# Five RMS norms on per-token sums in three columns, with the reciprocal spread by the tensor engine

## The reference

```python
def rms_norm(x, g):
    xf = x.astype(jnp.float32)
    y = xf * lax.rsqrt(jnp.mean(xf * xf, axis=-1, keepdims=True) + EPS)
    return (y * g.astype(jnp.float32)).astype(x.dtype)
```

## Time and profile before

| | |
|---|---|
| Runs | 2112.90, 2114.68, 2116.01 us; median 2114.68 |
| Profiled execution | 2114.53 us, span 2113.0 us |
| Mean granted clock of TensorE | 0.955 |
| Busy | PE 89%, PEld 81%, DVE 54%, ACT 41%, POOL 3% |
| Chain that ended last, by engine | PE 64%, issue 20%, DVE 10%, ACT 4%, DMA 1% |
| HBM | 115 GB/s over the span |

### The profile page before, as it was taken

How to read it: one execution, slowest core, us unless ns; L and a number is a source line. 1 busy time by engine, 2 the same in 40 slices (tenths; PEclk the granted TensorE clock), 3 DMA queues, 4 the chain that set the end, 5 groups by cost and what they waited for, 6 DMA issues and landing times.

```text
span 2113.0 us, 32355 instructions
## 1 busy us (share of the span) xinstructions
PE 1889.1 (89%) x11226; PEld 1703.9 (81%) x11226; DVE 1134.2 (54%) x1801; ACT 866.5 (41%) x1476; POOL 66.6 (3%) x72
## 2 busy tenths in 40 slices
PE   5977997789999989999989789977899997999995
PEld 3955897559969879999969478966698896999995
DVE  3667545673314477467365755366542246763754
ACT  3444433553322454344354354244533234543432
POOL 1000001000000000000000000011000000000000
PEclk9989999989999999999999899989999999999998
DMA  7410333113324443433353013321132345333331
GB/s 290 155 62 21 120 109 110 40 60 112 130 79 153 173 154 120 159 122 137 140 195 122 33 51 100 127 82 50 63 129 101 130 159 190 104 115 123 126 117 63
DMA packets 55967, 244.41 MB, mean 116 GB/s; under 512 B 6336, under 2 KB 6416, under 8 KB 52016
## 3 DMA queue, kind: packets, MB, share of 16 engines
q1 hardware_dynamic: 49824, 181.43, 25.3%
q0 software_dynamic: 6032, 61.52, 7.4%
HBM read 238.95 MB, written 3.96 MB: 115 GB/s over the span
## 4 chain that ended last, share of the span: by engine, by line
PE 64%; issue 20%; DVE 10%; ACT 4%; DMA 1%; POOL 0%; DVEq 0%; ACTq 0%; POOLq 0%
PE ps L1149 17%; PE ps L1150 17%; PE ps L1151 17%; PE ps L553 2%; PE ps L606 2%; PE ps L582 2%; DVE rstd L1563 1%; PE ps L620 1%; ACT w_hi L1327 1%; DVE wide L1567 1%; ACT region L741 1%; PE ps L473 1%; PE ps L501 1%; DMA region<-in_ada 1%; PE ps L440 1%
## 5 line engine op out<-in xcount | busy, mean ns | idle before, releaser
L1327 ACT ACTIVATE w_hi<-raw 128x1024 fp32r<-128x1024 f32 x344 | 365.0, 1061 | 897.1 <-PE ps L1151 897.1
L1149 PE MATMUL ps<-h_hi,w_hi 128*128 128x384 f32 x1632 | 557.0, 341 | 22.7 <-DVE h_lo L1555 21.9
L1150 PE MATMUL ps<-h_lo,w_hi 128*128 128x384 f32 x1632 | 553.6, 339 | 0.0
L1151 PE MATMUL ps<-h_hi,w_lo 128*128 128x384 f32 x1632 | 553.2, 339 | 0.0
L1551 DVE TENSOR_TENSOR w_lo<-raw,w_hi 128x1024 fp32r<-128x1024 f32 x248 | 327.2, 1319 | 414.0 <-ACT w_hi L1327 409.9
L1149 PE MATMUL ps<-in_hi,w_hi 128*128 128x384 f32 x992 | 344.0, 347 | 52.2 <-DVEq L377 28.4
L1150 PE MATMUL ps<-in_lo,w_hi 128*128 128x384 f32 x992 | 340.8, 344 | 0.0
L1151 PE MATMUL ps<-in_hi,w_lo 128*128 128x384 f32 x992 | 340.4, 343 | 0.0
L1149 PEld LDWEIGHTS ps<-h_hi,w_hi 128*128 128x128 f32 x1632 | 309.7, 190 | 26.8 <-issue 16.8
L1150 PEld LDWEIGHTS ps<-h_lo,w_hi 128*128 128x128 f32 x1632 | 309.9, 190 | 0.5 <-issue 0.3
L1151 PEld LDWEIGHTS ps<-h_hi,w_lo 128*128 128x128 f32 x1632 | 309.6, 190 | 0.0
(11 more groups left out here) (208 smaller groups left out, 1790.8 us busy)
## 6 DMA issues: line engine op xcount, KB each, us to landing
raw<-in_weights SPq DMA_DIRECT2D x346, 512.0 KB, 3.2
region<-in_ada POOLq DMA_DIRECT2D x20, 2048.0 KB, 9.6
wide<-in_ada POOLq DMA_DIRECT2D x2, 1536.0 KB, 7.3
region<-in_ada POOLq DMA_DIRECT2D x2, 1536.0 KB, 7.2
region<-in_consts POOLq DMA_DIRECT2D x2, 1152.0 KB, 5.6
region<-in_state POOLq DMA_DIRECT2D x2, 1024.0 KB, 11.7
region<-in_ada POOLq DMA_DIRECT2D x4, 512.0 KB, 8.5
out_state<-wide POOLq DMA_DIRECT2D x4, 512.0 KB, 2.9
```

Source lines behind the costliest of these rows:

```text
L1149: pe.matmul(out, ah, bh, start=start, stop=False)
L1150: pe.matmul(out, ah, bl, start=False, stop=False)
L1151: m = pe.matmul(out, al, bh, start=False, stop=stop)
L1327: act.activation(w_hi[:, j % AHEAD, :], raw[:, nxt, :], ACT.Copy).then_inc(hi_made.sem, 1)
```

## The change

Norms 1, 4, 5, 6 and 7 get another form; norms 2 and 3 stay. A squared block is now the stationary operand, 128 tokens at a time, and one column of ones streams past it: three matmuls a block, whose sums lie in three PSUM columns, with a token to each partition (`column_sums`). Root and reciprocal are taken on 128x3. Then TensorE multiplies a reciprocal column, broadcast along the free dimension as stationary operand, by the identity, three times 128 columns: this gives every partition the reciprocals of all tokens in a PSUM bank (`spread_rstd`). DVE multiplies with this bank instead of `rstd` in SBUF. Two signals are new, from DVE to TensorE (`rstd_cols_made`) and back (`rstd_spread`); DVE's own chain signal has five links fewer in a layer.

```diff
+        NORM_BANK = {1: 1, 4: 7, 5: 7, 6: 1, 7: 7}
+        def rstd_of(n):
+            return ps[:, NORM_BANK[n], 0:T] if n in NORM_BANK else rstd[:, :]
+        def sums_of(n):
+            return ps[:, NORM_BANK[n], T:T + CHUNKS]
+        root_cols, rstd_cols = stat[:, 0:CHUNKS], stat[:, CHUNKS:2 * CHUNKS]
         mod_cols = ps[:, 4, T:T + 16]
...
         roots = signal("roots", 7)
+        rstd_cols_made = signal("rstd_cols_made", 5)
+        rstd_spread = signal("rstd_spread", 5)
         side_in = [Signal(sem(f"side_in{i}"), 112) for i in range(2)]
...
+        def spread_at(signal_, L, n):
+            return signal_.at(L, (1, 4, 5, 6, 7).index(n) + 1)
         def settle(eng, mark):
...
+            def spread_rstd(L, n):
+                pe.wait_ge(rstd_cols_made.sem, spread_at(rstd_cols_made, L, n))
+                for c in range(CHUNKS):
+                    m = pe.matmul(rstd_of(n)[:, c * P:(c + 1) * P], rstd_cols[:, c:c + 1].broadcast_to([P, P]), ident,
+                                  start=True, stop=True)
+                m.then_inc(rstd_spread.sem, 1)
+            def column_sums(n, i, sq):
+                for c in range(CHUNKS):
+                    m = pe.matmul(sums_of(n)[:, c:c + 1], sq[:, c * P:(c + 1) * P], ones[:, 0:1], start=(i == 0 and c == 0),
+                                  stop=(i == DB - 1), skip_group_check=True)
+                return m
             def added_sum(L, which):
                 pe.wait_ge(added.sem, added.at(L, (which + 1) * (DB - 1)))
-                pe.matmul(ps[:, 7, 0:T], ones, mix[:, 0, :], start=True, stop=True).then_inc(sums.sem, 1)
+                for c in range(CHUNKS):
+                    m = pe.matmul(sums_of(4 + which)[:, c:c + 1], mix[:, 0, c * P:(c + 1) * P], ones[:, 0:1],
+                                  start=True, stop=True)
+                m.then_inc(sums.sem, 1)
+                spread_rstd(L, 4 + which)
...
                     pe.wait_ge(squares.sem, squares_at(L, n, i + 1))
-                    m = pe.matmul(ps[:, 7, 0:T], ones, sq[:, order[i], :], start=(i == 0), stop=(i == blocks - 1))
+                    if n in NORM_BANK:
+                        m = column_sums(n, i, sq[:, order[i], :])
+                    else:
+                        m = pe.matmul(ps[:, 7, 0:T], ones, sq[:, order[i], :], start=(i == 0), stop=(i == blocks - 1))
                     if i == blocks - 1:
                         m.then_inc(sums.sem, 1)
+                if n in NORM_BANK:
+                    spread_rstd(L, n)
...
                 act.wait_ge(sums.sem, sums.at(L, n))
-                act.activation(root[:, :], ps[:, 7, 0:T], ACT.Sqrt, scale=1.0 / width, bias=eps[:, 0:1])\
-                   .then_inc(roots.sem, 1)
+                out, total = (root_cols, sums_of(n)) if n in NORM_BANK else (root[:, :], ps[:, 7, 0:T])
+                act.activation(out, total, ACT.Sqrt, scale=1.0 / width, bias=eps[:, 0:1]).then_inc(roots.sem, 1)
...
                 dve.wait_ge(roots.sem, roots.at(L, n))
-                link(L, dve.reciprocal(rstd[:, :], root[:, :]))
+                if n in NORM_BANK:
+                    dve.reciprocal(rstd_cols, root_cols).then_inc(rstd_cols_made.sem, 1)
+                    dve.wait_ge(rstd_spread.sem, spread_at(rstd_spread, L, n))
+                else:
+                    link(L, dve.reciprocal(rstd[:, :], root[:, :]))
             def times_rstd(n, k, src):
-                dve.tensor_tensor(wide[:, k, :], src[:, k, :], rstd[:, :], ALU.mult).then_inc(scaled_by.sem, 1)
+                dve.tensor_tensor(wide[:, k, :], src[:, k, :], rstd_of(n), ALU.mult).then_inc(scaled_by.sem, 1)
...
-                times_rstd(L, 0, wide)
+                times_rstd(5 + 2 * which, 0, wide)
                 for k in range(DB):
                     if k + 1 < DB:
-                        times_rstd(L, k + 1, wide)
+                        times_rstd(5 + 2 * which, k + 1, wide)
                     dve.wait_ge(scaled_by.sem, scaled_by.at(L, (2 * which + 1) * DB + k + 1))
...
                 for k in range(DB):
-                    times_rstd(L, k, x)
+                    times_rstd(1, k, x)
                 vector(L, 1)
...
                     dve.scalar_tensor_tensor(out=wide[:, k, :], in0=wide[:, k, :], scalar=param("g_ssd", k),
-                                             in1=rstd[:, :], op0=ALU.mult, op1=ALU.mult).then_inc(y_value.sem, 1)
+                                             in1=rstd_of(4), op0=ALU.mult, op1=ALU.mult).then_inc(y_value.sem, 1)
                 y_los(L, 0, lambda k: wide[:, k, :])
...
                 for k in range(DB):
-                    times_rstd(L, k, x)
+                    times_rstd(6, k, x)
                 vector(L, 4)
```

More of the change, by code:

```diff
@@ L107 @@
 DOWN_LAST = ((3, 0, 1, 2, 4, 5, 7, 6), (7, 0, 1, 2, 3, 4, 5, 6))
-DVE_LINKS = 41
+DVE_LINKS = 36
 def build_program(nc, a_x, a_cond, a_state, a_ckv, a_kpe, a_params, a_consts, a_weights, a_ada,
```

## The result

The changed kernel takes 2120.09 us (median of 20 runs) and the kernel before 2111.19 (20 runs beside it); the ratio is 1.0043, 95% interval [1.0031, 1.0055], so the change costs 9.1 us by the ratio, with an interval of 6.5 to 11.6. The profiled execution has 2119.90 us, a span of 2118.3 and a mean granted clock of 0.945 instead of 0.955.

A forecast was written before the change was run, and what follows sets the result against it. TensorE was taken as the bound, a norm counting only through when the next stage's first operand is ready. Terms 5.1 - 4.6 + 3.2 + 6.9 + 1.7 = +12.3 on 2114.68 gave 2127 us, range 2117 to 2136.

The forecast's parts named there:

- Prices: New norm chain 1.5 us at 2.4 GHz, 2.1 at 1.2, against 3.24; new sums cost what the old did at either clock.
- the rival of the fixed time: Weight loads take a fixed time, so sums cost 0.68 us a block at either clock: -3.9, 2111 us; chance 0.04.
- The clock: TensorE loses full clock during column sums: five of norm 7's eight blocks at full clock, three of norm 6's.
- Norm 1, first layer: From the sums to vector 1: slower sums, then columns and sides queued behind the spreading, +5.1 us (0 to +7).
- the sums end at 33.9: Norm 1, first layer: the last three blocks cost 1.3 instead of 0.7 us, so sums end at 33.9, not 31.97.
- Norm 4: Both layers: shorter chain, gate tile fills TensorE's gap, branch's tile ends at 271.0 instead of 273.35: -2.3 us each.
- Norms 5 and 6: Both layers, to vector 4: products come earlier, but columns and side 9 follow the spreading and end last: +1.6 us each.
- Loop: Norm 7 and the next norm 1, to vector 1: slower sums, then sides 2 and 3 behind the spreading: +6.9 us.
- End: Norm 7, second layer, to the last transfer's issue: products later by +1.7 us (-1.4 to +3).
- The rival in which the clock holds: Loads count as activity and column sums keep 2.4 GHz: -9.4, 2105 us, loop still +3.8; chance 0.10.
- the queue behind the spreading: TensorE's columns, sides and first gate tile, queued behind the spreading, now wait for the chain they ran beside; loop +3.8 at full clock.

The follow-up runs named there:

- e3: Changed kernel with 128 columns of ones instead of one behind each weight load in norms 1, 6 and 7: 2097.07 us, ratio 0.9953 to the kernel before.
- e4: Changed kernel with the first group of column matmuls ahead of the spreading in norms 1, 6 and 7: 2114.61 us, ratio 1.0032 to the kernel before.
- e2: Changed kernel with only norms 1, 6 and 7 in the new form, norms 4 and 5 old: 2123.18 us, ratio 1.0089 to the kernel before.
- e6: Changed kernel with norm 1 alone in the new form, all others old: 2117.38 us, ratio 1.0042 to the kernel before.
- e10: Norm 7 alone in the new form, with 128 columns of ones and columns 11 ahead of the spreading: 2113.66 us, ratio 1.0018 to the kernel before.
- e7: On top of e3 and e4, norm 1's side 2 also ahead of the spreading: 2099.01 us, ratio 0.9953 to the kernel before.

## Why the prediction was right, step by step

The forecast of +12.3 us (2127) had the direction and the mechanism; measured were 2120.09, inside the range, and +9.1. Its base, three runs of the kernel before, lay 3.5 us above the median of twenty. Two of its five places came within 0.5 (norm 4, loop); norms 5 and 6 together were 3.0 too dear, norm 1 1.9, the end 0.8 too cheap. Point by point:

- *Prices*: right. The chain is 1.5 us at full clock; a spreading 0.94 or 1.65 (0.91 and 1.5 forecast); a block of column sums 0.67 and 1.28 (0.68 and 1.3 in the sums). Loads start 0.112 apart at full clock and 0.213 at half, so the rival of the fixed time fell. By the Trainium skill, TensorE: Matmul & The Clock Gate, section LDWEIGHTS (loading the stationary operand), a load takes its columns divided by 1.2 in ns, 107 for 128 columns, with no term for the clock. For these f32 records that is near the trace at full clock and half of it at half clock.
- *The clock*: right, and shown by e3: with 128 columns behind each load and the same loads the clock holds at 1.00, and the kernel is 19 us faster than the changed one. Where in the sums it falls was partly luck: three of norm 7's eight blocks were forecast at half clock, 22 of 48 records were (3.7 blocks), 7.80 us against 7.3; the same code took 5.96 in e4.
- *Norm 1, first layer*: +5.1 forecast, +3.2 in the trace and about +2.5 by the ten profiles. The failed step is "the sums end at 33.9": they end at 32.16. The forecast kept the old sums' stretch at half clock (26 to 28) and put three blocks at half clock behind it; in the trace there is one stretch, from 28 on, behind five blocks at full clock. In e2, e4 and e6 the clock fell earlier and the place is at +4.3 to +5.0. Chain, columns and sides behind the sums are as forecast (12.27 from the sums' end to vector 1, 12.4 forecast).
- *Norm 4*: -2.3 forecast, -2.6 and -1.7 measured, by another sum: the products came 1.1 and 1.0 earlier, not 1.7, since the spreading ran at half clock (1.65), and in the first layer the branch's tile gained 1.5, not 0.6, since all of its half-clock stretch fell on the gate tile. The gap of 3.9 us behind the gate tile is gone.
- *Norms 5 and 6*: the mis-sized term, +1.6 each forecast, -0.1 and +0.3 measured. In the first layer the sums themselves took what was forecast (8.48 us from 737.43 to 745.91, 8.5 forecast). They began 5.78 after the fifth sum began instead of 6.67, for columns 7 and side 8 ran partly at full clock (0.5 and 3.25 instead of 0.7 and 3.6); and from their end to vector 4 it took 7.44 instead of 8.2, mainly since columns 9 came at full clock again (0.61 for 1.1). That the columns end last, not the products, was right.
- *Loop*: +6.9 forecast, +7.3 measured, and by the forecast's way: vector 1 waits for the columns of sides 2 and 3, which run behind the spreading, and their loads are there (no wait at 1076.00). The size is luck in part, for two misses cancel: the next reciprocal came 26.2 us after norm 7's sums began, 24.8 forecast and 23.1 before, and the two sides took 5.34 instead of 6.4. What I had not seen is TensorE's own way round the loop; in the changed kernel it lies under the queue, but it alone costs +4.7 with norm 7's sums at full clock (e10). Norm 1's +5.3 (e6) and this +4.7 don't add up to the +7.3; that both wait for the same sides is how I read it, and no run shows it.
- *End*: +1.7 forecast, +2.5 measured: the sums took 2.9 longer, 1.85 forecast, and the chain gave back less than that.

The rival in which the clock holds is what e3 built: 2105 was its forecast, 9.4 us faster; e3 has 0.9953, 9.9 us faster, with norm 4 at -4.5 (-4.6 forecast), norms 5 and 6 at -3.5 twice (-3.6) and the end at -1.1 (-1.4). Its loop of +3.8 is there too, +3.6, but not for the reason given, the queue behind the spreading: e7 to e10 show side loads and parameters that come late.

## What to carry to other kernels

A shorter chain is worth its gain only where what is queued behind it on the engine that finishes it isn't what the next stage waits for: behind norm 4 stands a gate tile, behind norm 5 columns and a side product that the next products don't need, and these two, with one block to sum, gain 11 us alone; the three others took back more than that. Before work is turned from streaming into weight loads, look at the granted clock that it will get; a moving operand as wide as the load cost next to nothing (5.63 us against 5.52) and kept the clock here. In a loop over layers, a new wait near the end of an engine's body also delays what that engine needs to come round: look for the first instruction of the next turn, and count from the last wait.

## What was not expected

- TensorE shows as busy for 4.10 of 4.10 us and is granted 0.50 all the same, when it loads weights and streams single columns.
- 128 f32 columns behind each load cost next to no time: 48 records in 5.63 us, against 5.52 with single columns at full clock.
- From TensorE's last wait in the loop to its first matmul of the next turn it takes 3.8 to 4.4 us in thirteen of the fourteen profiles, whatever the wait is for, and 4.85 in e10.
